# Residual additions after two mixture-of-experts stages moved from VectorE to GpSimd

## The reference, cut to what matters

```
def rmsnorm(x, w):
    xf = x.astype(jnp.float32)
    y = xf * lax.rsqrt(jnp.mean(xf * xf, axis=-1, keepdims=True) + NORM_EPS)
    return (y * w.astype(jnp.float32)).astype(x.dtype)
...
    y = hier_moe(h, ...)                      # top-1 group, top-2 experts in it, plus a gated shared expert
    x = x + gt2 * rmsnorm(y, norm_w[i, 3])
```

## Time and profile before

| | us |
|---|---|
| median of 3 runs | 2982.31 (2976.86 to 2983.33) |
| the profiled execution's own time | 2967.23 |
| its span in the profile | 2965.4 |
| mean granted TensorE clock | 0.868 |

### The profile page before, as it was taken

How to read it: one execution, slowest core, us unless ns; L and a number is a source line. 1 busy time by engine, 2 the same in 40 slices (tenths; PEclk the granted TensorE clock), 3 DMA queues, 4 the chain that set the end, 5 groups by cost and what they waited for, 6 DMA issues and landing times. The chain is left out here.

```text
span 2965.4 us, 41692 instructions
## 1 busy us (share of the span) xinstructions
PE 2164.7 (73%) x17466; PEld 1530.0 (52%) x17466; DVE 1101.1 (37%) x1660; ACT 816.5 (28%) x1333; POOL 268.4 (9%) x268
## 2 busy tenths in 40 slices
PE   5978787779799479867666653899987866666552
PEld 4856565579577368833233221677775733233221
DVE  3266656554422254441011103566545431011103
ACT  4155555532122242321001002533322311000001
POOL 2021111110110100010000001011101010000001
PEclk8988898889799789988788776999998888888787
DMA  8355555423688333289999996211111589999995
GB/s 318 100 171 178 166 176 164 164 44 124 240 318 326 132 100 100 86 332 417 384 420 413 404 410 244 66 49 44 44 44 49 194 344 408 409 411 416 406 412 195
DMA packets 218831, 698.39 MB, mean 236 GB/s; under 512 B 24365, under 2 KB 123382, under 8 KB 161782
## 3 DMA queue, kind: packets, MB, share of 16 engines
q1 hardware_dynamic: 195446, 625.04, 55.8%
q0 software_dynamic: 12992, 33.10, 3.2%
q10 hardware_dynamic: 10176, 37.23, 3.1%
HBM read 664.34 MB, written 45.11 MB: 239 GB/s over the span
## 5 line engine op out<-in xcount | busy, mean ns | idle before, releaser
L220 PE MATMUL PS<-ring,arena 128*32 128x256 f32 (+5 forms) x7584 | 810.3, 496 | 514.8 <-DMA ring<-in_moe_w_up 181.7
L220 PEld LDWEIGHTS PS<-ring,arena 128*32 128x32 f32 (+3 forms) x7584 | 421.5, 140 | 855.3 <-issue 696.8
L220 PE MATMUL PS<-second 128*128 128x256 f32 (+1 forms) x4416 | 792.3, 338 | 31.6 <-DVE second L239 29.9
L220 PEld LDWEIGHTS PS<-second 128*128 128x128 f32 x4416 | 670.6, 194 | 142.3 <-issue 27.1
L232 ACT ACTIVATE arena<-PS 128x512 f32<-128x512 f32 (+1 forms) x314 | 155.9, 497 | 1091.1 <-PE PS L220 953.2
L239 DVE TENSOR_TENSOR arena<-arena,PS 128x256 f32<-128x256 f32 (+1 forms) x83 | 43.4, 523 | 767.9 <-PE PS L220 767.6
L220 PE MATMUL PS<-arena 128*64 128x64 f32 (+8 forms) x1504 | 280.9, 368 | 26.9 <-DVE arena L250 10.6
L232 ACT ACTIVATE arena<-arena 128x512 f32<-128x512 f32 (+6 forms) x271 | 195.8, 723 | 299.4 <-DVE arena L239 150.9
L220 PEld LDWEIGHTS PS<-arena 128*128 128x128 f32 (+5 forms) x1504 | 174.3, 190 | 135.2 <-issue 107.2
L258 DVE COPY arena<-PS 128x512 f32<-128x512 f32 (+4 forms) x169 | 93.5, 553 | 403.8 <-PE PS L220 345.5
L228 PE MATMUL PS<-ident,arena 128*128 128x128 f32 x919 | 140.8, 302 | 139.0 <-ACT arena L232 89.3
(11 more groups left out here) (157 smaller groups left out, 1111.0 us busy)
## 6 DMA issues: line engine op xcount, KB each, us to landing
ring<-in_moe_w_gate SPq DMA_DIRECT2D x148, 1024.0 KB, 10.4
ring<-in_moe_w_up SPq DMA_DIRECT2D x148, 1024.0 KB, 13.1
ring<-in_moe_w_down SPq DMA_DIRECT2D x148, 1024.0 KB, 11.2
ring<-in_ada_w SPq DMA_DIRECT2D x48, 1024.0 KB, 5.3
y_d<-arena ACTq DMA_DIRECT2D x51, 512.0 KB, 8.4
ring<-in_w_mod SPq DMA_DIRECT2D x24, 1024.0 KB, 6.2
ring<-in_gdn_in_w SPq DMA_DIRECT2D x32, 512.0 KB, 4.1
ring<-in_hg_w_in SPq DMA_DIRECT2D x24, 512.0 KB, 6.9
```

What stands on the lines that cost most here:

```text
L220: return P.e.matmul(o, l, r, start=st, stop=sp)
```

## The change

DVE's `post_ve` keeps the scaling `stt` and now marks it as `post`. The addition to x becomes a POOL instruction of the same shape in a new function `post_gp`, which waits for `post`, adds and marks `x`. It is called for the four tiles after the eight indirect DMAs of m1 and of m2, eight additions in all. The waiters for `x` (ACT) now wait for POOL's count instead of DVE's. m0 is as before.

```diff
     def post_ve(name, t):
         V.wait_ge(at("sq", name, t))
-        stt(XN[:, t, :], XN[:, t, :], rs[:, t:t + 1], GROW, ALU.mult, ALU.mult)
-        tt(x[:, t, :], x[:, t, :], XN[:, t, :], ALU.add, "x", name, t)
+        stt(XN[:, t, :], XN[:, t, :], rs[:, t:t + 1], GROW, ALU.mult, ALU.mult, "post", name, t)
+
+    def post_gp(name, t):
+        G.wait_ge(at("post", name, t))
+        gtt(x[:, t, :], x[:, t, :], XN[:, t, :], ALU.add, "x", name, t)
...
                 bounds_check=m.NY - 1, oob_is_err=False).then_inc(*state["comb"][i].next("comb", m.i, i))
+        if m.i:
+            for t in range(4):
+                post_gp(f"m{m.i}", t)
```

## The result

| | before | after |
|---|---|---|
| median of 20 runs each | 2978.85 us | 2987.47 us |
| ratio, 95% interval | | 1.0021 (1.0012 to 1.0031), +3.6 to +9.2 us |
| profiled execution, its span | 2965.4 | 2986.7 |

The change makes the kernel slower by a little. The forecast was +7.6.

What follows compares the result with a forecast made beforehand. The prediction took DVE to bound the tail behind m2, and x(3) to delay ACT and PE behind m1. +4.2 us behind m2 and +3.4 behind m1 made +7.6 on the median 2982.31: 2989.9 us, range 2980 to 2997.

Steps and rivals of the forecast that it cites:

- The length of the addition: Each 1024-column addition on POOL takes 2.40 us, extrapolated from full-input rows of 512 and 768 columns; 1.22 on DVE before.
- case (a): Rival: POOL's addition costs only 1.90 us, with the same exclusion; +3.6 us, 2985.9 us; chance 0.12.
- Exclusion: In both tails, POOL additions and DVE `stt` with two SBUF inputs run in turn; +0.98 us for each of three tiles.
- Case (e): Rival: additions take 2.5 us on POOL and nothing overlaps at hand-overs; +9.2 us, 2991.5 us; chance 0.08.
- case (d): Rival: DVE, not POOL, starts first behind each scaling `stt`; +7.0 us, 2989.3 us; shares the forecast's chance of 0.64.
- The 0.47 of idleness on DVE behind m1: DVE's idle stretch ahead of mix(3) behind m1 would lie under POOL's addition, taking 0.47 us off the cost there.
- M2: Behind m2, end of tile 0's scaling `stt` to end of the last addition; predicted +4.2 us.
- M1: Behind m1, end of tile 0's scaling `stt` to PE's start on the transposes; predicted +3.4 us.
- Passing on in full: The delay of x(3) behind m1, less ACT's 0.33 us lateness, reaches the program's end whole: +3.4 us.
- Case (c): Rival: the delay behind m1 is absorbed downstream, as by m2's weight stream; +4.2 us, 2986.5 us; chance 0.08.
- The end of the program: From DVE's last addition behind m2 to the end: one store, 3.04 us; no added cost was forecast there.
- case (b): Rival: an `stt` does not exclude POOL; -0.4 us behind m1, -1.6 behind m2, 2980.3 us; chance 0.08.

Runs made afterwards that it cites:

- idle_adds: Kernel before, DVE keeping its additions, plus a POOL addition of dead tiles released by each scaling `stt`, awaited by nobody; +14 us against before (8.9 to 18.4).
- idle_fills: As idle_adds, with two POOL memsets of 1024 columns in place of each idle addition; +4 us against before (0.0 to 8.3).
- psum_one: The changed kernel, with only the first `stt` of mix(2) and mix(3) reading the shared expert's tile from PSUM; +21 us against before (16 to 26).
- late_fill: Kernel before, plus one POOL memset of a single column behind m2's last addition, awaited by nobody; +6 us against before (0.3 to 10.7).
- again: The changed kernel run once more, unaltered, beside other runs of before; ratio 1.0034 (1.0021 to 1.0047), +10 us (6.2 to 14.0).
- delay_m1: The changed kernel, with eight idle POOL additions ahead of tile 3's addition behind m1; +33 us against before (25 to 41).
- m2_only: The change made behind m2 alone, DVE keeping the additions behind m1; +6 us against before (2.1 to 10.7).
- m1_only: The change made behind m1 alone, DVE keeping the additions behind m2; +6 us against before (1.8 to 9.2).
- psum_all: The changed kernel, with ACT copying GROW and shared expert's tiles 2 and 3 into PSUM, where the `stt` read them; +15 us against before (9 to 21).

## Why the prediction was right, and where it was not

**The length of the addition.** 2.40 predicted, 2.33 measured. The line through the rows with full inputs was the right choice, the nearer row in size (1.90) the wrong one; case (a) falls.

**Exclusion.** Right, and shown from both sides: an addition on POOL excludes and a memset does not (idle_adds against idle_fills), and an `stt` on DVE is held up with two SBUF inputs and not with one (psum_one). The hand-over gives back 0.20, not 0.14: DVE's `stt` ends 1.08 behind POOL's addition. So each of three tiles costs 3.50 from `stt` to `stt` where 3.63 was predicted: +0.85, not +0.98. Case (e), 2.5 on POOL and no overlap, falls with the same rows, though its +9.2 happens to lie nearer to the whole than the forecast.

**Who goes first.** POOL by 0.02 behind tiles 0 and 1, as in the earlier trace rows, and by 0.31 behind tile 2, where `sq` comes late but inside POOL's addition, as the prediction had it; case (d) did not arise.

**The 0.47 of idleness on DVE behind m1.** Here a step failed. It was to vanish under POOL's addition. After, it stands one instruction later, at 1840.97 (0.47, where 0.10 is usual), out of POOL's shadow, and a like one of 0.46 has come behind m2 (2971.45). It belongs to a place in DVE's stream and not to chance: behind m1 it is 0.47 in all fourteen profiles, ahead of mix(3) where DVE keeps its additions (before, late_fill, idle_adds) and between the two `stt` of mix(3) where POOL has them; behind m2 it is 0.46 in after, again and delay_m1 alike, stands ahead of post(1) in m2_only (2953.44) and has come ahead of mix(3) in m1_only, which is why M2 is 15.12 there and not 14.75. What makes it, no run settled. Where it does fall under a POOL addition it vanishes as predicted: in idle_adds M1 grows by 3 x 1.89 - 0.33 - 0.37 = 5.0. The prediction also took too much for it: 0.11 of the 0.47 was already in its sum as the usual gap, so 0.36 should have gone. In the change nothing goes behind m1, and 0.37 comes behind m2. With the smaller cost of a tile this cancels: M1 3 x 0.85 + 1.16 - 0.33 = +3.4 (3.4 predicted), M2 3 x 0.85 + 0.37 + 1.16 = +4.1 (4.2 predicted). That both sums came out so near is luck in part.

**Passing on in full.** Right as far as the totals can tell: m1_only excludes 0, and delay_m1 passes at least 14 of 19.3. Case (c) falls; that 1 or 2 us of the 3.4 are absorbed is not excluded.

**The end of the program.** The missing term, and the largest error. I took 3.04 us from the last addition to the end as fixed, since it was read as store and landing, and did not ask what else closes behind an engine that is given new last work. It is +3.6 (6.7 against 3.1). A row for it was there before: POOL's DRAIN of 17.7 us, over at 2954.9, some 10 us ahead of the end, with POOL idle since 2945.7. That row would have given 9.2 from POOL's last work to the end of the DRAIN, where an addition at the end gives 6.5; it shows the term, not its size. So the prediction's sum should have been +11.2, and 2993.5 on its base. That the first comparison came out at +6.3, near the +7.6 on record, is chance of measurement on top of a missing term; the second, +10.1, is nearer to the whole. The 11.1 stand on the stretches, which repeat to 0.05, and not on the totals.

**The case (b)** as the change stands was wrong, but its numbers were tested by psum_all: -0.4 behind m1 as computed, -1.2 instead of -1.6 behind m2, the difference being the 0.37 again.

## What to carry to other kernels

Before an elementwise step with two inputs is moved from VectorE to GpSimd, look at what VectorE does beside it. Here, where those instructions had two SBUF inputs, the two engines ran in turn, and the slower one set the pace; with one input moved to PSUM they ran side by side, and even then the gain was 0.4 and 1.2 us. One SBUF input is not enough as a rule: the `tensor_scalar` of the earlier trace rows has only one and was held up. Before work is moved to GpSimd near the end of a program, look at when its closing DRAIN ended: it becomes part of the path. Where totals scatter by more than the effect, stretches between two named instructions can repeat to hundredths, as M1, M2 and End did here, and can be summed; what lies between them cannot be read so.

## What the runs showed of the hardware that I had not expected

GpSimd's closing DRAIN ended 6.47 us behind its last instruction in the eleven profiles in which that was an addition (2.34 us) or a memset (0.95 or 0.10), and the program ended 6.71 behind it in ten of them; behind indirect DMAs it took 9.2 to 10.6. A `tensor_scalar` on VectorE with one SBUF tile as input took 2.2 us beside a GpSimd addition and 0.62 alone. Memsets of 1024 columns on GpSimd (0.95 each) ran beside VectorE instructions with two SBUF inputs with no stretch on either side. And `stt` on VectorE with an operand, or operand and result, in PSUM took 1.28 to 1.29, no more than from SBUF.
